# An expert stage with 88 places instead of 96, and scatter and turning in 64-column strips

## The reference

```python
D_MODEL, SEQ, N_EXPERTS, TOP_K, D_FF_EXPERT = 1024, 256, 8, 2, 3584

def swiglu(t, w1, w3, w2):
    return (jax.nn.silu(t @ w1) * (t @ w3)) @ w2

def moe_swiglu(x, router, w1, w3, w2):
    t = x.reshape(bsz * seq, d)
    logits = (t @ router).astype(jnp.float32)
    top_val, top_idx = lax.top_k(logits, TOP_K)
    probs = jax.nn.softmax(top_val, axis=-1)
    combine = jnp.sum(jax.nn.one_hot(top_idx, N_EXPERTS) * probs[..., None], axis=1)
    out = jnp.zeros((bsz * seq, d), jnp.float32)
    for e in range(N_EXPERTS):
        out = out + combine[:, e:e + 1] * swiglu(t, w1[e], w3[e], w2[e])
    return out
```

## Time and profile before

| | |
|---|---|
| time, median of 3 runs | 2139.74 us (2136.3 to 2143.62) |
| the profiled execution's own time | 2140.0 us |
| its span from first to last instruction | 2137.6 us |
| expert stage: TensorE's first `gather` to its last `down` | 1140.3 to 2113.4 us |
| mean granted TensorE clock over the span | 0.965 |

### The profile page before, as it was taken

The page is one execution under the profiler, slowest core; times in us unless marked ns, Lnnn a source line. Parts: engine busy times, 40 slices in busy tenths (PEclk is TensorE's granted clock), DMA queues, the critical chain, the costliest instruction groups (busy, mean ns, idle before and its releaser), DMA issues.

```text
span 2137.6 us, 64607 instructions
## 1 busy us (share of the span) xinstructions
PE 1990.7 (93%) x29738; PEld 1758.3 (82%) x29738; DVE 697.9 (33%) x1434; ACT 327.5 (15%) x745; POOL 101.7 (5%) x44
## 2 busy tenths in 40 slices
PE   8998788889998999878888999999999999999996
PEld 7777777567776788767657999999999999999996
DVE  7963564312111783563422111111111111111113
ACT  3222222011001322321201000000000000000001
POOL 4400000001000420000000000000000000000000
PEclk9999999899999999989889999999999999999998
DMA  7233111334443333210163999999999999999991
GB/s 285 89 119 118 61 42 41 130 115 148 147 147 138 119 118 119 98 42 22 60 246 148 357 359 376 354 369 364 360 375 361 358 364 375 364 358 363 368 371 68
DMA packets 54475, 470.99 MB, mean 220 GB/s; under 512 B 5184, under 2 KB 5456, under 8 KB 20336
## 3 DMA queue, kind: packets, MB, share of 16 engines
q1 hardware_dynamic: 37744, 292.04, 36.4%
q10 hardware_dynamic: 16272, 175.07, 21.3%
q0 software_dynamic: 368, 2.64, 0.4%
HBM read 468.68 MB, written 1.05 MB: 220 GB/s over the span
## 4 chain that ended last, share of the span: by engine, by line
PE 49%; DVE 1%; issue 0%; ACT 0%; DVEq 0%
PE bank L1000 28%; PE bank L923 14%; PE bank L951 2%; PE bank L800 1%; PE bank L990 1%; PE bank L904 1%; PE bank L785 0%; PE bank L435 0%; DVE x_tok L1746 0%; PE bank L865 0%; PE bank L744 0%; PE bank L983 0%; PE bank L971 0%; DVE arena L1741 0%; PE bank L959 0%
## 5 line engine op out<-in xcount | busy, mean ns | idle before, releaser
L1000 PE MATMUL bank<-arena,ring 128*64 128x96 f32 x8192 | 359.7, 246 | 0.0
L1000 PEld LDWEIGHTS bank<-arena,ring 128*64 128x64 f32 x8192 | 345.7, 137 | 0.0
L1000 PE MATMUL bank<-arena 128*64 128x96 f32 x6144 | 264.8, 246 | 0.9 <-DVE arena L1891 0.9
L1000 PEld LDWEIGHTS bank<-arena 128*64 128x64 f32 x6144 | 257.2, 137 | 2.5 <-issue 2.5
L1859 DVE TENSOR_TENSOR arena<-arena,bank 128x96 f32<-128x96 f32 x224 | 56.4, 252 | 561.6 <-ACT arena L1252 561.6
L771 PE MATMUL bank<-xT,ring 128*128 128x256 f32 x1024 | 229.1, 384 | 0.0
L771 PEld LDWEIGHTS bank<-xT,ring 128*128 128x128 f32 x1024 | 195.6, 192 | 32.3 <-issue 5.5
L1252 ACT ACTIVATE arena<-bank 128x96 f32<-128x96 f32 (+1 forms) x246 | 64.5, 262 | 995.2 <-PE bank L1000 801.9
L923 PE MATMUL bank<-arena,ring 128*64 128x96 f32 x4096 | 192.7, 247 | 1.3 <-issue 1.3
L923 PEld LDWEIGHTS bank<-arena,ring 128*64 128x64 f32 x4096 | 176.0, 137 | 12.1 <-issue 12.1
L450 PE MATMUL bank<-xT,ring 128*128 128x256 f32 x736 | 164.8, 386 | 3.4 <-DMA ring<-in_w_in 3.4
(11 more groups left out here) (417 smaller groups left out, 1791.8 us busy)
## 6 DMA issues: line engine op xcount, KB each, us to landing
ring<-in_moe SPq DMA_DIRECT2D x66, 1536.0 KB, 8.4
ring<-in_moe ACTq DMA_DIRECT2D x62, 1536.0 KB, 8.9
arena<-in_moe SPq DMA_DIRECT2D x49, 1536.0 KB, 8.9
arena<-in_moe ACTq DMA_DIRECT2D x47, 1536.0 KB, 9.3
ring<-in_ffn SPq DMA_DIRECT2D x22, 1536.0 KB, 6.5
ring<-in_w_gate SPq DMA_DIRECT2D x32, 1024.0 KB, 5.0
ring<-in_w_in SPq DMA_DIRECT2D x14, 1536.0 KB, 6.6
ring<-in_w_branch SPq DMA_DIRECT2D x8, 1024.0 KB, 4.8
```

The costliest lines, as they stand in the source:

```text
L1000: last = mm(bank[c:c + STRIP, g * CAP:(g + 1) * CAP], w[:, at:at + STRIP], rhs[:, kt, :], start=(kt == 0), stop=(kt == KT - 1), skip_group ...
```

## The change

`CAP` goes from 96 to 88. Every matmul of `hidden`, `down` and `gather` so has 88 moving columns instead of 96, and ScalarE's and VectorE's operations on these results have 88 columns per group. The stage is passed through once if no expert has more than 88 tokens, twice up to 176, three times above.

Three steps that used the array with more than 64 stationary columns are written in strips of 64: the turn of `y_cols` and of `selw` becomes `turn`, an ordinary matmul with the identity moving and 64 columns of the source stationary, and the scatter takes 64 columns of `selwT` at a time. `y_cols` and `selw` are 128 columns wide for that, the columns above 88 zero. `turn_y` stays for the last expert.

```diff
-CAP = 96
+CAP = 88
...
-        ys_part, x_cols, y_cols = area(14372, 2 * P), area(14628, TT, 2 * P), area(15140, 2, CAP)
+        ys_part, x_cols, y_cols = area(14372, 2 * P), area(14628, TT, 2 * P), area(15140, 2, P)
...
-        sel, selw, selwT = area(15396, TT, CAP), area(15588, TT, CAP), area(15780, T)
+        sel, selw, selwT = area(15396, TT, CAP), area(18640, TT, P), area(15780, T)
...
+                def turn(bank, at, src):
+
+                    for c in range(0, P, STRIP):
+                        last = mm(bank[c:c + STRIP, at:at + P], src[:, c:c + STRIP], ident, start=True, stop=True)
+                    return last
...
-                    turn_y(banks[6], 2 * P, y_cols, range(2)).then_inc(S["y_turned"], 1)
+                    for n in range(2):
+                        last = turn(banks[6], (2 + n) * P, y_cols[:, n, :])
+                    last.then_inc(S["y_turned"], 1)
...
                     for tt in range(TT):
-                        last = mm(banks[5][:, tt * 2 * P:(tt + 1) * 2 * P], selwT[0:CAP, tt * P:(tt + 1) * P],
-                                  ys_part[0:CAP, :], start=True, stop=True)
+                        for c in range(0, P, STRIP):
+                            last = mm(banks[5][c:c + STRIP, tt * 2 * P:(tt + 1) * 2 * P],
+                                      selwT[0:CAP, tt * P + c:tt * P + c + STRIP], ys_part[0:CAP, :], start=True,
+                                      stop=True)
...
-                        last = nc.tensor.transpose(banks[6][0:CAP, tt * P:(tt + 1) * P], selw[:, tt, :], ident)
+                        last = turn(banks[6], tt * P, selw[:, tt, :])
...
-                                nc.scalar.copy(y_cols, yT[:, 1 - e % 2, 2 * b:2 * b + 2, :])\
+                                nc.scalar.copy(y_cols[:, :, 0:CAP], yT[:, 1 - e % 2, 2 * b:2 * b + 2, :])\
...
+                nc.vector.memset(y_cols[:, :, CAP:P], 0.0)
                 choose(0)
```

More of the change, by code:

```diff
@@ L1829, in choose @@
                         if e:
-                            ins = ts(selw[:, tt, :], C("cap"), rank9[:, tt, e - 1:e], weight9[:, tt, e - 1:e],
+                            ins = ts(selw[:, tt, 0:CAP], C("cap"), rank9[:, tt, e - 1:e], weight9[:, tt, e - 1:e],
                                      ALU.is_equal, ALU.mult)
```

## The result

The changed kernel takes 2052.5 us (2051.42 to 2053.97, four runs) against 2138.02 us (2135.38 to 2143.62, four runs) of the kernel before, measured beside it: a ratio of 0.9597, 95% interval 0.9576 to 0.9619, or 81 to 91 us less. The forecast was 2053 us. The span fell from 2137.6 to 2050.2 us.

The account below looks back on a forecast made before the run. The prediction took TensorE to bound the kernel, the DMAs fed by it. 74.0 + 0.2 (first gather) + 10.9 + 1.9 + 0.5 = 87.5 us off 2140.0 gave 2052.5, say 2053 us; range 2047 to 2073.

Parts of the forecast that it names:

- TensorE is the bound, and stays it: Expert stage: TensorE sets the pace and the DMAs are fed by it, before and after; chance 0.70, at 2053 us.
- Fewer columns: Expert-stage matmul records, 8 moving columns fewer: 3.36 ns less a record, 2.31 us a block, 74.0 us over 32 blocks.
- The lower bound, 0.37: Price of a moving column in ns, from records 64 and 96 columns wide; it would make the columns' gain 66 us.
- The scatter: Scatter of each block in strips: 0.87 us instead of 1.21 with the width change, 10.9 us over 32 blocks.
- The turn: Turn of y_cols in each block, in strips: 0.44 us instead of 0.50, 1.9 us over 32 blocks.
- `turn_selw`: Turn of selw once an expert, in strips: 0.06 us less each, 0.5 us over 8.
- The sum: All gains together, 87.5 us, taken from the profiled execution's 2140.0 us: 2052.5, say 2053 us.
- Whether the weights keep up: Expert-stage weight loads: 217 loads need 393 GB/s; taken as sufficient, since queued loads ahead of the stage moved 428.
- The DMAs as the bound: Rival in the expert stage: weight loads set the pace, 2064 us at 388 GB/s or 2092 at 376; chance 0.18.
- The record that does not get shorter: Rival: 41.25 ns is the price of weight loading or issue, only the strips' 13.3 us stay, 2127 us; chance 0.05.
- TensorE and the DMAs slow each other: Expert stage: both nearly full, they might slow each other at the higher rate; no size or chance given.
- A second pass: Rival: an expert with more than 88 tokens runs the stage again, 881 us more, 2934 us; chance 0.03.

Follow-up runs that it names:

- the places alone: Kernel before with CAP 88 instead of 96 and no strips for scatter and turns: 2066.19 us against 2139.15, ratio 0.9662.
- with 80 and with 72: Changed kernel with CAP 80 or 72 instead of 88, one pass forced, the fullest expert's last tokens left out: 1999.2 us and 1993.46 us.
- the half loads: Changed kernel, each of the 217 later weight loads bringing only half its columns, matmuls unchanged: 2055.65 us, ratio 0.9594.

## Why the prediction was right

**TensorE is the bound, and stays it.** Right. It is busy in every microsecond of the stretch after the change, and halving the DMAs' work changed nothing.

**Fewer columns: 3.36 ns a record, 74.0 us.** Measured with the places alone: 2.28 us a block or 3.31 ns a record, and 73 us. The width's price was bounded by runs at 64 and at 512 columns, and it was the wide one that was near: from 96 to 72 columns a pair of records goes from 82.5 to 62.5 ns, 0.417 ns a column and record. The wide run gives the same figure when its starts are taken, which are 429.3 ns apart (the 431.7 of the forecast have the end of the last record in them): (214.6 − 41.25) / 416 = 0.417. The lower bound, 0.37, came from the 64-wide run, and the forecast's doubt about it names the wrong reason: at the change of line its records follow at the same 55 ns as within a line. They come 58.4 ns a pair throughout, where 2.5 + 0.833 × 64 would be 55.8; why was not tried, and their 64 rows are the other difference that the forecast names.

**The scatter: 0.34 us a block, 10.9 us.** 1.06 + 0.15 became 0.86 + 0.01. **The turn: 0.06 us a block, 1.9 us.** 0.35 + 0.15 became 0.44. By distance between blocks the strips gave 0.42 together instead of 0.40.

**`turn_selw`: 0.06 us an expert.** Off, by half a microsecond over all: it takes 0.51 us and the records behind it 4.88 instead of 4.85. With the turn between them the blocks lie 0.51 us further apart, as before the change. Its second pair of records begins 155 ns after the first, where the other turn has 109, and the first pair of `hidden` behind it is followed after 101 ns instead of 76; why was not tried.

**The sum.** 2.69 us a block over 32 blocks are 86.1 us; the stage is 86.4 shorter, the span 87.4, of which 1.0 lies ahead of and behind the stage. Forecast 87.5. That 2053 came within 1 us of the time is partly luck: the forecast subtracted from 2140.0, the profiled execution, while the median of the kernel before was 2138.02 in the result. By medians the change gives 85.5 us, 2 less than forecast, and that the interval of 81 to 91 cannot tell apart.

**Whether the weights keep up.** Right, and the reason given holds. The rate per busy share, 388 GB/s before, was not a ceiling: 397 at a share of 0.98 after the change is 405, and where loads are always queued it is 426 at 1.01, or 422, with the 426 within half a percent of the 428 read just ahead of the stage. The packets of the traces show what moves it. Each is 12 KB and usually takes some 462 ns. Between 1180 and 2000 us, 9.6% of them took more than 550 ns before the change, 0.9 us in the mean, 5.7% after it, 4.0% with 85 places, and under 0.2% with 80 and with 72, where loads queue. Before the change 39% of the packets were that long in the first microsecond after a queue had been empty, and 6% otherwise. The 393 GB/s needed were there with 8% to spare. At 88 places the queues were not yet in the state that the forecast counted on, with a landing time of 9.3 to 10.0 us, and did not need to be; it came with 80. The 400 GB/s forecast for the profile were 397 over the stretch and 401 from 1300 to 1500 us. The Trainium skill's 358 GB/s ("DMA: Bandwidth & Descriptors", section "Where 436 GB/s comes from") is passed by the stage of every kernel here that brings whole loads, 361 to 426; no run had the pair's other core loading.

**The rivals.** The DMAs as the bound is real, but further down: it begins between 85 places (413 GB/s from 1300 to 1500 us with the blocks 88 columns apart, no waits) and 80. The record that does not get shorter is excluded down to 72 columns. That TensorE and the DMAs slow each other, where the forecast would have been most wrong, is excluded for the stage by the half loads. A second pass cost 851 us with 84 places, where the forecast had 881 for the 27.4 us blocks of 88; with 88 there was one, 217 loads from 1150 us on.

## What to carry to other kernels

Where two resources are both over 90% busy, find which one waits, and then take the other one's ceiling from a stretch in which its queue is never empty: its rate per busy share in a stretch where it is fed one request at a time was too low here, 388 against 422. Price a narrower matmul by long runs at other widths, not by its own time divided by its columns, and count the steps that change the stationary width: each return to strips cost 0.15 us here. When a size is trimmed to odd numbers, keep the distance between operand blocks at a multiple of 16 bytes: it gave 0.18 us a block here. 85 places in blocks 88 columns apart, 2029.56 us, are the fastest version found that gives every token its places in one pass; with these inputs none is to spare.

## What the runs showed of the hardware

In `hidden` and `down`, matmuls on two strips of 64 stationary columns by turns, a pair of float32 records starts every 82.5 ns with 96 moving columns, 75.8 with 88, 73.3 with 85 and 62.5 with 72: 2.5 ns and 0.833 for each column. The first pair on a moving operand that does not begin at a multiple of 16 bytes took 3 to 5 ns longer in `hidden` with 85 and 86 places; the following pairs on the same operand did not, and some of them came 0.8 ns early. In `down` the same showed as 2 to 3 ns in units 2, 3 and 5 of the 85 places with blocks 88 apart, and not in the two kernels whose `hidden` had it already. Why only the first pair pays, and why `down` differs, was not tried. Loads of 1536 KB from two queues move 388 GB/s per unit of busy share when each queue holds about one (217 loads of 8.9 us each, on two queues in 940 us), and 422 when each holds two to three (18.5 us each, in 810 us). In one profiled run the granted clock fell from 1.00 to 0.50 for 3.4 us right behind an idle time of TensorE of 1.93 us.
